# A hybrid decoder step on one core: VectorE's mixer work in another order

## The reference

```
ua, va, xb, gb, uc, gl = split(h @ w_in)
A: ya = gelu(ua) * (tril(W_s) layernorm(gelu(va)) + b)       per 128 positions
B: xc = conv4(xb); hs = real gated recurrence(xc); yb = hs * gelu(gb)
C: x_t = a x_{t-1} + (b_bar u_t),  y = Re(C x) + D u         32 groups, 64 complex states
   z = gelu(y); yc = z * sigmoid(z @ glu_w + glu_b)
out = (sum_k sigmoid(gl_k + b_gate_k) * (branch_k @ w_branch_k)) @ w_out
```

## Time and profile before

| | |
|---|---|
| median of 3 runs | 1450.63 us (1450.41 to 1464.84) |
| profiled execution | 1451.03 us |
| its span | 1449.3 us |
| TensorE matmul busy | 1320.0 us, 91% |
| VectorE busy | 985.8 us, 68% |
| ScalarE busy | 690.0 us, 48% |
| mean granted TensorE clock | 0.947 |

### The profile page before, as it was taken

The page is one execution under the profiler, slowest core; times in us unless marked ns, Lnnn a source line. Parts: engine busy times, 40 slices in busy tenths (PEclk is TensorE's granted clock), DMA queues, the critical chain, the costliest instruction groups (busy, mean ns, idle before and its releaser), DMA issues.

```text
span 1449.3 us, 23175 instructions
## 1 busy us (share of the span) xinstructions
PE 1320.0 (91%) x9162; PEld 1284.4 (89%) x9162; DVE 985.8 (68%) x1302; ACT 690.0 (48%) x787; POOL 63.9 (4%) x117
## 2 busy tenths in 40 slices
PE   4785789999999999898869999999999999999995
PEld 4774789999999999797769989999999999999994
DVE  6799943466655555489872445648888888788873
ACT  4254122344443243345522334557667667666561
POOL 2000500100000000000210200000000000000000
PEclk9897799999999999999989999969999999999998
DMA  6320573545655346132474534538788787787850
GB/s 215 106 88 30 122 171 107 130 153 173 202 162 166 121 155 205 58 106 88 104 121 141 144 114 147 218 125 319 284 308 316 264 336 292 286 319 282 309 224 38
DMA packets 47456, 262.64 MB, mean 181 GB/s; under 512 B 6048, under 2 KB 6624, under 8 KB 34832
## 3 DMA queue, kind: packets, MB, share of 16 engines
q1 hardware_dynamic: 42048, 243.55, 48.6%
q0 software_dynamic: 4752, 15.37, 5.9%
q10 hardware_dynamic: 576, 2.62, 0.4%
HBM read 255.89 MB, written 5.62 MB: 180 GB/s over the span
## 4 chain that ended last, share of the span: by engine, by line
PE 77%; DVE 15%; DMA 3%; ACT 2%; issue 2%; DVEq 0%; SPq 0%; ACTq 0%
PE bank L1836 22%; PE bank L1838 22%; PE bank L1837 22%; DMA raw<-w_in_in 3%; DVE w_lo L1083 2%; PE s_bank L2081 2%; PE bank L2081 1%; PE bank L1848 1%; PE bank L1827 1%; ACT w_hi L766 1%; PE bank L1954 1%; PE s_bank L1954 1%; DVE cross L1320 1%; PE s_bank L2117 0%; PE bank L1949 0%
## 5 line engine op out<-in xcount | busy, mean ns | idle before, releaser
L1089 DVE TENSOR_TENSOR mw_lo<-mraw,mw_hi 128x2816 fp32r<-128x2816 f32 x96 | 295.8, 3088 | 61.3 <-ACT mw_hi L773 60.3
L1836 PE MATMUL bank<-hn_hi,w_hi 128*128 128x320 f32 x656 | 220.3, 336 | 54.9 <-DVE w_lo L1083 42.1
L773 ACT ACTIVATE mw_hi<-mraw 128x2816 fp32r<-128x2816 f32 x96 | 245.0, 2552 | 16.1 <-PE bank L1838 16.0
L1083 DVE TENSOR_TENSOR w_lo<-raw,w_hi 128x1024 fp32r<-128x1024 f32 x128 | 154.4, 1223 | 93.4 <-ACT w_hi L766 90.3
L1837 PE MATMUL bank<-hn_lo,w_hi 128*128 128x320 f32 x656 | 214.3, 327 | 0.0
L1838 PE MATMUL bank<-hn_hi,w_lo 128*128 128x320 f32 x656 | 213.7, 326 | 0.0
L1836 PEld LDWEIGHTS bank<-hn_hi,w_hi 128*128 128x128 f32 x656 | 133.8, 204 | 62.7 <-DVE w_lo L1083 46.7
L1836 PE MATMUL bank<-mw_hi,x_hi 128*128 128x352 f32 x512 | 168.7, 330 | 1.9 <-DVE x_lo L1700 1.9
L1838 PE MATMUL bank<-mw_hi,x_lo 128*128 128x352 f32 x512 | 165.8, 324 | 0.0
L766 ACT ACTIVATE w_hi<-raw 128x1024 fp32r<-128x1024 f32 x128 | 132.8, 1052 | 69.3 <-PE bank L1838 47.7
L1837 PE MATMUL bank<-mw_lo,x_hi 128*128 128x352 f32 x512 | 165.2, 323 | 0.0
(11 more groups left out here) (443 smaller groups left out, 2820.1 us busy)
## 6 DMA issues: line engine op xcount, KB each, us to landing
mraw<-w_moe_in SPq DMA_DIRECT2D x96, 1408.0 KB, 7.2
raw<-w_in_in SPq DMA_DIRECT2D x88, 512.0 KB, 4.3
uraw<-w_gu_in SPq DMA_DIRECT2D x44, 512.0 KB, 3.5
raw<-w_br_in SPq DMA_DIRECT2D x24, 512.0 KB, 3.9
uraw<-w_dn_in SPq DMA_DIRECT2D x16, 704.0 KB, 4.1
raw<-w_wo_in SPq DMA_DIRECT2D x16, 512.0 KB, 3.5
toep<-k_scratch POOLq DMA_DIRECT2D x16, 256.0 KB, 11.9
pl<-pl_in POOLq DMA_DIRECT2D x2, 1840.0 KB, 8.3
```

The lines of the kernel that those rows point to most:

```text
L773: act.activation(mw_hi[c % MSPLIT][:, :], mraw[slot][:, :], ACT.Copy).then_inc(hi_ready, 1)
L1083: dve.tensor_tensor(w_lo[g % SPLIT][:, :], raw[slot][:, :], w_hi[g % SPLIT][:, :].bitcast(F32), ALU.subtract).then_inc(lo_ready, 1)
L1089: dve.tensor_tensor(mw_lo[c % MSPLIT][:, :], mraw[c % MRAW][:, :], mw_hi[c % MSPLIT][:, :].bitcast(F32), ALU.subtract).then_inc(lo_ready, 1)
L1836: pe.matmul(out, w_h[k], x_h[k], start=start and k == 0, stop=False)
```

## The change

Constants of slots:

```diff
-ST_TRANS, ST_K, ST_U, ST_INJECT, ST_T, ST_Y, ST_Z, ST_GLU = 1, 3, 5, 7, 9, 12, 17, 20
+ST_TRANS, ST_K, ST_INJECT, ST_Y, ST_GLU = 2, 12, (14, 16), 18, 23
```

Before, the injections and states stood in slots 7 and 8, k in 3, the outputs in 12 and 14, the GLU in 20. VectorE, ahead of the slots:

```diff
                 chain(dve.tensor_tensor(row(R_NR), row(R_NR), row(R_C1), ALU.add))
+                split(0, 3)
...
                 chain(dve.tensor_copy(a[1][:, :, 1], row(R_AI)))
+                split(0, 4)
...
                     chain(dve.tensor_tensor(bcomp[c][:, :, :], t[2 * c], t[2 * c + 1], op))
+                split(l, 5 if l == 0 else 4)
                 (bbar copies)
-                split(l, 4)
-                (six products of h0 with a power)
-                split(l, 5)
+                def ahead(): (the same six)
+                split(l, 6 if l == 0 else 5)
...
-                input_powers(0, (6, 7))
+                input_powers(0, (7, 8))
...
-                split(l, 8)
+                split(l, 10)
                 (statistics of v)
-                output_powers(0, (9, 10))
                 split(l, 12)
-                (normalising of v, in line)
-                input_powers(1, (13, 14))
+                def normalised(between): (the same, between(b) before each b)
```

VectorE, in the slots (conv's inner split goes from 15 to 16):

```diff
-                    if s == 1:
-                        output_powers(1, (16, 16))
-                    if s == 2 and l == 0:
-                        turns(lambda w: None)
+                    if s == 0:
+                        input_powers(1, (15, 15))
+                    if s == 2:
+                        normalised(lambda b: split(l, 16 + b // 2))
+                    if s == 8:
+                        output_powers(0, (upto(0, 1), upto(0, 1)))
+                    if s == 9:
+                        output_powers(1, (upto(0, 2), upto(0, 2)))
+                    if s == 10:
+                        ahead()
+                    if s == 11 and l == 0:
+                        turns(lambda w: split(l, upto(0, {0: 4, 2: 4, 4: 4, 8: 5, 16: 5}[w])))
                         router_low()
                     if s == ST_K:
                         k_diag()
-                    if s in (ST_INJECT, ST_INJECT + 1):
-                        states(s - ST_INJECT)
-                    if s == ST_GLU + 1:
-                        glu()
-                    if s == ST_GLU + 3:
-                        (y_low of the four yc tiles)
-                    if s == 0:
+                    if s in ST_INJECT:
+                        states(ST_INJECT.index(s))
+                    if s == 1:
                         (wait for x_b) conv()
                     if s == 5:
                         lru()
+                glu()
                 for m in range(KD):
                     split(l, upto(2, m))
+                    if m == 0:
+                        (y_low of the four yc tiles)
                     branch(2, m)
```

The rotations in `turns`, for E of 32 columns:

```diff
                 for _ in range(3):
-                    chain(dve.tensor_tensor(t, cs, cs, ALU.mult))
-                    chain(dve.tensor_tensor(t2, sn, sn, ALU.mult))
-                    chain(dve.tensor_tensor(t3, cs, sn, ALU.mult))
-                    chain(dve.tensor_tensor(cs, t, t2, ALU.subtract))
-                    chain(dve.tensor_tensor(sn, t3, t3, ALU.add))
+                    chain(dve.scalar_tensor_tensor(t, sn, -2.0, sn, ALU.mult, ALU.mult))
+                    chain(dve.scalar_tensor_tensor(sn, cs, 2.0, sn, ALU.mult, ALU.mult))
+                    chain(dve.tensor_scalar(cs, t, 1.0, None, ALU.add))
+                between(0)
...
-                w = 2
+                w = 1
                 while w < NP:
-                    (five operations that square column w // 2 into t, t2)
+                    v = min(w, NP - 1 - w)
...
+                    lo, hi = slice(1, v + 1), slice(w + 1, w + 1 + v)
+                    pr, pi = (e[:, :, w:w + 1].to_broadcast(full) for e in (er, ei))
                     (six operations, on v columns)
```

Queues and the other engines:

```diff
 GpSimd
-                (wait for k, its write) at the head of the layer's list
+                (wait for k, its write) after pool.sem_inc(ends_read, 1), ahead of the Toeplitz loads
-                pool.wait_ge(z_ready, KB * (l + 1))
                 for i in range(4):
+                    pool.wait_ge(z_ready, KB * l + 2 * (i // 2) + 2)
 ScalarE
-                turn(0)
                 for m in range(KB):
+                    if m == 2:
+                        turn(0)
...
+                        if s == 4:
+                            act.wait_ge(v_ready, l + 1)
...
-                    if s == ST_GLU + 2:
-                        (four copies yc -> yc_hi)
+                (four copies yc -> yc_hi) after the last slot
 TensorE
-                turn(0)
                 for m in range(KB):
+                    if m == 2:
+                        turn(0)
                     project(("xb", l, m))
...
-                    if s in (ST_INJECT, ST_INJECT + 1):
-                        inject(s - ST_INJECT)
+                    if s in ST_INJECT:
+                        inject(ST_INJECT.index(s))
```

More of the change, by code:

```diff
@@ L928, in _ @@
                                            bias=sm("glu_b", l, m, t=half)).then_inc(a_free, 1)
-                    if s == ST_GLU + 2:
-                        for m in range(KB):
-                            act.wait_ge(yc_ready, KB * l + m + 1)
-                            act.activation(yc_hi[:, m], yc[:, m], ACT.Copy).then_inc(y_hi_ready, 1)
+                for m in range(KB):
+                    act.wait_ge(yc_ready, KB * l + m + 1)
+                    act.activation(yc_hi[:, m], yc[:, m], ACT.Copy).then_inc(y_hi_ready, 1)
                 def acc_high(m):
@@ L1238, in turns @@
                 chain(dve.tensor_copy(ei[:, :, 1], sn))
[L1239 removed]
+                w = 1
                 while w < NP:
[L1242 to L1252 removed]
+                    v = min(w, NP - 1 - w)
+                    if v <= 0:
+                        break
+                    lo, hi = slice(1, v + 1), slice(w + 1, w + 1 + v)
+                    full = [P, DEPTH * NST, v]
+                    pr, pi = (e[:, :, w:w + 1].to_broadcast(full) for e in (er, ei))
+                    tt = cross[:, :, :].rearrange("p s n -> p (s n)")[:, 0:DEPTH * NST * v].rearrange("p (n w) -> p n w", w=v)
                     chain(dve.tensor_tensor(er[:, :, hi], er[:, :, lo], pr, ALU.mult))
@@ L1258, in turns @@
                     chain(dve.tensor_tensor(ei[:, :, hi], ei[:, :, hi], tt, ALU.add))
+                    if w > 1:
+                        between(w)
                     w *= 2
-                    between(w)
             def router_low():
@@ L1365, in _, with normalised @@
                         dve.bn_aggr(mv[0:w, b], bnst[0:w, b]).then_inc(var_ready, 1)
-                output_powers(0, (9, 10))
                 split(l, 12)
-                dve.wait_ge(std_ready, l + 1)
-                dve.wait_ge(ln_loaded, 32 * (l + 1))
-                chain(dve.reciprocal(lnr[:, :], lnr[:, :]))
-                for b, w in enumerate((P, P, P)):
-                    vt = v_tok[0:w, b]
-                    chain(dve.tensor_scalar(vt, vt, mv[0:w, b, 0:1], lnr[0:w, b:b + 1], ALU.subtract, ALU.mult))
-                    chain(dve.tensor_tensor(vt, vt, ln_rows[0:w, 0], ALU.mult))
-                    if b < 2:
-                        chain(dve.tensor_tensor(vt, vt, ln_rows[0:w, 1], ALU.add))
-                    else:
-                        dve.tensor_tensor(vt, vt, ln_rows[0:w, 1], ALU.add).then_inc(v_ready, 1)
-                dve.wait_ge(v_ready, l + 1)
-                input_powers(1, (13, 14))
+                def normalised(between):
+                    dve.wait_ge(std_ready, l + 1)
+                    dve.wait_ge(ln_loaded, 32 * (l + 1))
+                    chain(dve.reciprocal(lnr[:, :], lnr[:, :]))
+                    for b, w in enumerate((P, P, P)):
+                        between(b)
+                        vt = v_tok[0:w, b]
+                        chain(dve.tensor_scalar(vt, vt, mv[0:w, b, 0:1], lnr[0:w, b:b + 1], ALU.subtract, ALU.mult))
+                        chain(dve.tensor_tensor(vt, vt, ln_rows[0:w, 0], ALU.mult))
+                        if b < 2:
+                            chain(dve.tensor_tensor(vt, vt, ln_rows[0:w, 1], ALU.add))
+                        else:
+                            dve.tensor_tensor(vt, vt, ln_rows[0:w, 1], ALU.add).then_inc(v_ready, 1)
+                    dve.wait_ge(v_ready, l + 1)
                 def k_diag():
@@ L1452, in conv @@
                         if k == 1:
-                            split(l, 15)
+                            split(l, 16)
                     dve.sem_inc(xc_ready, 1)
@@ L1546, in _ @@
                         k_diag()
-                    if s in (ST_INJECT, ST_INJECT + 1):
-                        states(s - ST_INJECT)
-                    if s == ST_GLU + 1:
-                        glu()
-                    if s == ST_GLU + 3:
-                        for m in range(KB):
-                            y_low(yc[:, m], yc_hi[:, m], yc_lo[:, m], 3 + m)
```

(8 more changed lines are left out.)

34 lines of the change are left out of this document (12 added, 22 removed).

## The result

The changed kernel takes **1522.14 us** (median of 5 runs, 1520.91 to 1529.65), the kernel before 1450.63 (5 runs): ratio 1.0479, 95% interval 1.0442 to 1.0516. That is 71.5 us slower, where 36.4 were forecast, and outside the range, which ended at 1504. The direction was right and most waits came within 3 us of the forecast; the size was half.

What follows compares the result with a forecast made beforehand. VectorE was taken to bound each layer's mixer early and to have room late. Layer 0 at +10.8 us and layer 1 at +25.1 gave +35.9 on the profiled 1451.0: 1487 us, range 1450 to 1504.

Steps and rivals of the forecast that it cites:

- clock term of the sum: Lower clock around TensorE's waits: 1.0 us at the start, 2.6 in slots 0 to 7, 3.6 in 8 to 16.
- The GLU's chain: Before the third group's first branch: 9.1 us of chain against 3.5 of gate projection, 5.6 wait and 0.5 for the clock.
- The start: Layer 0's projections: the 9.7 us wait before the fourth goes, 3.2 idle comes next; gain 11 us, layer 1 about 2.
- Slots 0 to 7: TensorE waits 2.0 us on input powers, 4.0 on conv, 4.5 before slot 8, which ends at 137.3.
- Slots 8 to 16: TensorE waits 2.9, 1.5, 5.4, 4.0 and 4.7 us on VectorE; the second injection ends at 209.6 before SyncE's addition.
- SyncE: GLU weight loads wait for k and hold up later weights: +6.4 us in layer 0, +0.9 in layer 1.
- (a) Toeplitz loads: Before the output products: loads take 24.5 us from the second injection, two slots cover 10.5, so 14.1 of delay.
- (b) z: Before the GLU: z is loaded 24.7 us after the outputs end, three slots cover 15.8, so 8.9 of delay.
- Rival 1: Split and raw buffers let look-ahead absorb VectorE's blocks in the front: 1417 us if all is won; chance 0.13.
- Rival 2: The Toeplitz loads hide, the wait shrinks to 4.4 us, 9.7 off each layer: 1468 us; chance 0.10.
- Rival 3: Front waits won by half and z path at its lower bound, so both ends cancel: 1452 us; chance 0.12.
- Rival 4: SyncE's hold-up spreads, later loads bunch and the clock is down in every wait: +15, 1502 us; chance 0.15.

Runs made afterwards that it cites:

- b_fill: The kernel before with spare matmuls on TensorE ahead of its own waits for VectorE: 1448.15 us, ratio 0.9970.
- a_fill_full: The changed kernel with spare matmuls covering the whole of three waits a layer (Toeplitz loads, z, third group's first low halves): 1504.36 us, ratio 1.0362.
- a_fill_all: The changed kernel with a_fill_full's spare matmuls and more ahead of the front waits for VectorE: 1487.60 us, ratio 1.0264.
- b_start: The kernel before with only two weight splits put between the constants and powers of layer 0 on VectorE: 1449.12 us, ratio 0.9975.
- a_glu_later: The changed kernel with a layer's two GLU weight loads 12 weight chunks later in SyncE's order: 1517.89 us, ratio 1.0435.
- b_tail: The kernel before with only the GLU's products in slot 23 instead of 20 and its later chain: 1469.68 us, ratio 1.0151.
- b_turns_late: The kernel before with b_start's two splits and shorter turns moved behind the recurrence, with splits inside: 1452.37 us, ratio 1.0004.
- a_fill: The changed kernel with 44, 38 and 34 spare matmuls ahead of the waits for Toeplitz loads, z and yc's low halves: 1512.06 us, ratio 1.0413.
- b_turns: The kernel before with only the change's shorter turns, in their old place in slot 2: 1449.25 us, ratio 0.9984.

## Why the prediction was wrong, by its own steps

**The failing step is the clock term of the sum.** It charged 0.5 to 1.0 us per wait (1.0 at the start, 2.6 for slots 0 to 7, 3.6 for slots 8 to 16, 0.5 in the GLU's chain), and 9 us for the first outputs. Layer 0, forecast and measured:

| stretch | forecast us | measured us |
|---|---|---|
| to the end of slot 8 (time) | 137.3 | 142.5 |
| to the second injection's end (time) | 216.0 | 226.3 |
| to the first outputs | 24.6 | 23.8 |
| first outputs | 9 | 16.05 |
| slots 19, 20 and second outputs | 19.5 | 20.6 |
| z | 24.7 | 24.0 |
| GLU and first branch | 20.1 | 23.2 |

That is 20.0 us too little; layer 1 is 20.7 (5.3 to the second injection, then 0.7, 7.1, 4.0, -0.9, 4.5). These are of the slowest execution; by medians the whole miss is 35.1 us. Idle time was not the error. The forecast's waits in layer 0 add up to 67.2 us (38.6 to the second injection, 14.1, 8.9, 5.6); measured are 308.3 - 244.8 = 63.5. So it left 288.6 - 67.2 = 221.4 us of busy TensorE for matmuls that had taken 230.7 before, in a layer with more waits. It came out at 244.8. The 23.4 us above the sum's 221.4 lie in every stage: 3.2 up to the end of slot 8, 5.3 to the second injection, 1.9 to the first outputs, 7.1 in them, 1.1, 1.9 and 3.1 in the three stages behind. That check needed no run: a layer with more idle time than before and 9 us less busy time, for the same matmuls, needed a reason, and the sum gave none.

The price was read too low as well. Behind the waits of 3.3 us and more, a gate's 24 matmuls and weight loads took 5.1 to 6.6 us for 3.7, and first outputs 16 for 8.5. The trace of before had it: the projection behind the 9.7 us wait took 6.5 us for 3.7.

```profile
48.21:54.70 6.49, 6.49 (x26) 6.49 (x27) 6.15 (x13) 0.00 (x0) 0.00 (x0) 0.54 0.66 198
```

It had the outputs' loss too: 9.8 us for 8.4 in layer 1, with no wait ahead. I had kept most of that loss on the side of before and counted the new one at the size of a short stall. b_fill shows the second half of the error: the old loss was nearly free (3.8 us), since it lay ahead of places that VectorE sets; about half of the new one (17.8 us, a_fill_full) lies behind transfers and in the tail, where nobody takes it back.

The Trainium skill (TensorE: Matmul & The Clock Gate, What's actually happening) puts the penalty of coming up to speed at under 1% of a typical kernel's span; it speaks there of a kernel's first matmuls. Here the penalty comes again behind wait after wait: a_fill_all won back 34.5 of 1522 us, 2.3%, and b_fill 3.8 of 1452, 0.3%.

**The other steps.**
- *The start*: the 9.7 us wait went in the changed kernel, and 3.2 us stood behind it, as forecast. x_b ended at 80.5 for 79.3. Right there; on the base of before (b_start) it was passed on.
- *Slots 0 to 7*: waits of 2.0 and 3.9 for 2.0 and 4.0, then 5.65 for 4.5. Right to 1.2 us.
- *Slots 8 to 16*: waits of 3.3, 0.4, 4.3, 0.5, 12.1, 4.1 for 2.9, 1.5, 5.4, 0, 10.4 (4.0 and SyncE's 6.4), 4.7. Right.
- *SyncE*: a_glu_later takes 7.9 us off the wait (12.12 to 4.23), for 6.4 forecast. Right.
- *(a) Toeplitz loads*: 14.1 us of idle forecast, 11.4 measured in layer 0, and the first outputs' clock was missed (7 us a layer). Wait 2.7 us too long, consequence wrong.
- *(b) z*: 8.9 forecast, 6.4 measured, and slower matmuls in the slots between filled the rest, so the stage's 24.0 us for 24.7 is in part luck. (c) *The GLU's chain*: 5.6 forecast and 5.6 measured; b_tail has 5.5.
- *Rival 1* (look-ahead absorbs VectorE's blocks) fell: low halves cost 63.4 us. *Rival 2* fell: the loads took 24 us from the injection. *Rival 3* fell for the changed kernel, but b_start and b_turns_late show idle time passed on where VectorE bounds. *Rival 4* named the clock and gave it, with SyncE's hold-up, 0.15 and 15 us where 35 were missing: the clock was the right mechanism, at less than half its size, and SyncE's part was as charged.

What would have shown the forecast right (waits of about 10, 9 and 6 in the tail, one in slot 14 that ends with a weight load) did show, but shorter in two places: 7.2 and 8.6 for the 10, 6.4 and 6.5 for the 9. Those signs could not see a missed clock. A sign on busy time would have.

## What to carry to other kernels

Cost a new TensorE wait as two terms: its idle time, and the matmuls behind it at the lower clock, read from the same kind of wait in the trace; check the sum of busy time against that of before. Then ask who takes the loss back: here it was nearly free ahead of the blocks of the bounding engine, and was paid behind transfers and at the tail. Where a wait for a transfer stays, spare matmuls ahead of it can be worth more than shortening it: here those at three waits gave 17.8 us, earlier injections 12. Size them to the wait: too few left 1.4 us of idle, too many held TensorE up by 2 to 4 us (a_fill).

## What the hardware showed that I had not expected

- The output products (40 columns each) didn't bring the clock back: 16.05 us at 0.50 in both layers, busy all the time, against 8.5 when they began and stayed at full clock.
- The same products lost a full clock while TensorE was busy: 2 and 6 us after their start in a_fill, 6.7 us after it in layer 1 of the kernel before. In a_fill_full they kept it for all of their 8.5 us.
- So a projection right behind them ran at 0.68 (b_fill, 5.3 us) or 0.55 (b_turns, 6.3), with no idle time in between. In b_fill the outputs' matmuls are at full speed up to 214.5, and those from 214.7 on are slow:

```profile
206.35:214.70 8.35, 8.35 (x102) 7.95 (x100) 0.49 (x1) 0.00 (x0) 0.00 (x0) 1.00 0.27 105
214.72:220.04 5.32, 5.32 (x28) 5.32 (x27) 1.23 (x1) 1.38 (x2) 0.00 (x0) 0.68 0.23 74
```

- Spare matmuls beside the Toeplitz loads (DMA share 1.00) delayed them by little: from the second injection's end to the outputs it was 23.75 us in the changed kernel and 24.3 in a_fill.
